# Second layer's first gate product set: S1 moved to second place, with T1's low part made from even tiles and a kept copy

## The reference, cut to what matters

```python
def rmsnorm(x, g):
    xf = x.astype(jnp.float32)
    y = xf * lax.rsqrt(jnp.mean(xf * xf, axis=-1, keepdims=True) + EPS)
    return (y * g.astype(jnp.float32)).astype(x.dtype)

def ffn_half(x, g, wg, wu, wd):
    h = rmsnorm(x, g)
    return x + 0.5 * ((jax.nn.silu(h @ wg) * (h @ wu)) @ wd)
...
def layer(h, pos, cache, ...):
    h = ffn_half(h, n1, w1g, w1u, w1d)
    z = rmsnorm(h, nm) @ w_in
    m, st = token_mix(z, ...)
    h = h + m @ w_out
    h = ffn_half(h, n2, w2g, w2u, w2d)
```

## Time and profile before

| | |
|---|---|
| median of 3 runs | 2104.92 us |
| profiled execution, and its span | 2107.2 us, 2105.4 us |
| granted clock of TensorE over the span | 0.992 |
| TensorE busy | 2054.5 us, 98% |
| VectorE busy | 1675.6 us, 80% |
| ScalarE busy | 978.2 us, 46% |
| GpSimd busy | 362.7 us, 17% |
| the place of the change | 1056 to 1074 us of the span |

### The profile page before, as it was taken

One profiled execution on the slowest core, in us unless ns is written; L12 is line 12 of the kernel. 1 busy time (PEld: TensorE's weight loads), 2 busy tenths in 40 slices (PEclk: granted clock), 3 DMA queues, 4 the chain that ended last, 5 costly groups with the idle time before them and its releaser, 6 DMA issues. The chain is left out here.

```text
span 2105.4 us, 41112 instructions
## 1 busy us (share of the span) xinstructions
PE 2054.5 (98%) x15435; PEld 1980.3 (94%) x15435; DVE 1675.6 (80%) x2481; ACT 978.2 (46%) x1772; POOL 362.7 (17%) x219
## 2 busy tenths in 40 slices
PE   8999999999999999999989999999999899999998
PEld 7999999999778999999989999999987699999998
DVE  5999997655655999998889999975555579999975
ACT  6544453324435544463465555433354364444532
POOL 0322200141110222200022221002402112222000
PEclk9999999999998999999999999999999999999999
DMA  4323323351111233322223322325312013332331
GB/s 130 96 84 100 97 73 104 94 129 40 44 42 61 83 98 100 94 87 84 76 81 99 100 82 88 98 76 130 94 42 63 31 61 101 100 99 78 94 93 63
DMA packets 236727, 178.35 MB, mean 85 GB/s; under 512 B 35808, under 2 KB 231616, under 8 KB 236608
## 3 DMA queue, kind: packets, MB, share of 16 engines
q1 hardware_dynamic: 231712, 170.36, 27.1%
q10 hardware_dynamic: 4896, 6.36, 1.1%
HBM read 170.12 MB, written 3.62 MB: 83 GB/s over the span
## 5 line engine op out<-in xcount | busy, mean ns | idle before, releaser
L1431 PE MATMUL pair<-t_parts,chunk_high 128*128 128x288 f32 x4592 | 916.8, 295 | 6.3 <-POOL chunk_low L794 2.6
L1431 PEld LDWEIGHTS pair<-t_parts,chunk_high 128*128 128x128 f32 x4592 | 736.7, 188 | 8.0 <-POOL chunk_low L794 3.2
L1431 PE MATMUL pair<-t_parts,chunk_low 128*128 128x288 f32 x2296 | 677.8, 295 | 0.0
L1431 PEld LDWEIGHTS pair<-t_parts,chunk_low 128*128 128x128 f32 x2296 | 431.4, 188 | 0.0
L794 POOL TENSOR_TENSOR chunk_low<-set_raw,chunk_high 128x512 fp32r<-128x512 f32 x164 | 240.6, 1477 | 869.6 <-ACT chunk_high L893 869.6
L893 ACT ACTIVATE chunk_high<-chunk_sum 128x512 fp32r<-128x512 f32 x328 | 203.8, 630 | 371.8 <-DVE chunk_sum L1982 190.4
L788 POOL TENSOR_TENSOR w_low<-raw,w_high 128x1024 fp32r<-128x1024 f32 (+2 forms) x48 | 114.7, 2394 | 626.8 <-ACT w_high L841 626.8
L1994 DVE TENSOR_TENSOR chunk_low<-chunk_sum,chunk_high 128x512 fp32r<-128x512 f32 x328 | 214.6, 695 | 9.3 <-ACT chunk_high L893 1.9
L1378 PE MATMUL pair<-hidden_high,w_high 128*128 128x288 f32 x896 | 193.6, 298 | 6.5 <-DVE hidden_low L2257 6.4
L1378 PE MATMUL pair<-hidden_high,w_low 128*128 128x288 f32 x896 | 191.8, 296 | 0.0
L1378 PE MATMUL pair<-hidden_low,w_high 128*128 128x288 f32 x896 | 191.6, 295 | 0.0
(11 more groups left out here) (300 smaller groups left out, 3742.1 us busy)
## 6 DMA issues: line engine op xcount, KB each, us to landing
set_raw<-in_w_up_dram SPq DMA_DIRECT2D x44, 1024.0 KB, 5.3
set_raw<-in_w_gate_dram SPq DMA_DIRECT2D x44, 1024.0 KB, 5.3
raw<-in_w_down_dram SPq DMA_DIRECT2D x64, 448.0 KB, 3.8
down_raw<-in_w_down_dram SPq DMA_DIRECT2D x16, 1024.0 KB, 5.4
raw<-in_w_in_dram SPq DMA_DIRECT2D x20, 512.0 KB, 4.0
raw<-in_w_in_dram SPq DMA_DIRECT2D x16, 256.0 KB, 3.8
raw<-in_w_out_dram SPq DMA_DIRECT2D x8, 512.0 KB, 3.5
raw<-in_w_out_dram SPq DMA_DIRECT2D x16, 256.0 KB, 4.0
```

What stands on the lines that cost most here:

```text
L1431: mm = nc.tensor.matmul(out, c[:, j, p, :], tr[p // 2][:, seat(p), x, t, :], start=p == 0 and n == 0, stop=p == KP - 1 and n == 2)
```

## The change

Three edits, all for the one set where `first` holds. TensorE goes through the products in the order A11, S1, A12, S2, S3, S4, A22. ScalarE and VectorE wait for three used chunks instead of two or three where they want A12's or S1's chunk buffer. And VectorE's list in `down_to_gate_up` is written anew: S1 and S2 are summed, T1 of the last pair is copied into the place of its T2 and its low is made, and S1's low is made, all before `plain_out(7)`; `odd_sums` then reads T1 from the copy.

```diff
--- before.py
+++ after.py
@@ -102,6 +102,12 @@
 PRODUCTS = {A11: (B11, ALONE, None), A12: (B21, FIRST, 0), S1: (T1, SECOND, 0), S2: (T2, FIRST, 1),
             S3: (T3, SECOND, 1), S4: (B22, THIRD, 0), A22: (T4, THIRD, 1)}
 C11, C12, C21, C22, U2, U4, U3, P1 = range(8)
+FIRST_ORDER = [A11, S1, A12, S2, S3, S4, A22]
+
+
+def used_after(j, first):
+
+    return 3 if first and j in (A12, S1) else j + 1
 
 
 def is_plain(layer, w):
@@ -535,6 +541,7 @@
         d_low = sem("down_chunk_low")
         d_left, d_out, d_scaled, h_part = sem("down_left"), sem("down_out"), sem("down_scaled"), sem("h_part")
         dt_sum, dt_high, dt_ready = sem("down_t_sum"), sem("down_t_high"), sem("down_t_ready")
+        t1_kept = sem("t1_kept")
         h_by_act, plain_low = sem("h_by_act"), sem("plain_low")
 
         def stand_alone(eng):
@@ -926,7 +933,7 @@
                     last = isinstance(i, int) and i == MP - 1 and b == 1
 
                     def done(j):
-                        act.wait_ge(chunk_used, 7 * q + (j + 1))
+                        act.wait_ge(chunk_used, 7 * q + used_after(j, opens and b == 0))
 
                     done(A11)
                     if last:
@@ -1403,7 +1410,7 @@
                     opens = isinstance(i, int) and i == 0
                     first = opens and b == 0
                     after_plain = isinstance(i, int) and i == 1 and b == 0 and is_plain(layer, w)
-                    for j in range(7):
+                    for j in FIRST_ORDER if first else range(7):
                         t, pair, half = PRODUCTS[j]
                         if j in (A11, A12):
                             pe.wait_ge(low_by_pool, 2 * q + {A11: 1, A12: 2}[j])
@@ -2003,13 +2010,13 @@
                 nc.vector.scalar_tensor_tensor(out=tf[p // 2][:, seat(p), 1, T1, :], in0=h[:, 2 * p, HALF:], scalar=gain_of(gain_col + 2 * p), in1=tf[p // 2][:, seat(p), 1, B11, :] if x is None else x,
                                                op0=ALU.mult, op1=ALU.subtract).then_inc(t_sum, 1)
 
-            def odd_sums(ph, p, gain_col, x=None):
+            def odd_sums(ph, p, gain_col, x=None, t1=None):
 
                 n = ph * (4 * KP) + 4 * p
                 x21, x22 = (tf[p // 2][:, seat(p), 1, B21, :], tf[p // 2][:, seat(p), 1, B22, :]) if x is None else x
                 dve.wait_ge(t_odd, ph * KP + (p + 1))
                 dve.wait_ge(t_sum, n + 1)
-                nc.vector.tensor_tensor(tf[p // 2][:, seat(p), 1, T2, :], x22, tf[p // 2][:, seat(p), 1, T1, :], ALU.subtract).then_inc(t_sum, 1)
+                nc.vector.tensor_tensor(tf[p // 2][:, seat(p), 1, T2, :], x22, tf[p // 2][:, seat(p), 1, T1, :] if t1 is None else t1, ALU.subtract).then_inc(t_sum, 1)
                 dve.wait_ge(t_sum, n + 2)
                 nc.vector.tensor_tensor(tf[p // 2][:, seat(p), 1, T4, :], x21, tf[p // 2][:, seat(p), 1, T2, :], ALU.subtract).then_inc(t_sum, 1)
                 nc.vector.scalar_tensor_tensor(out=tf[p // 2][:, seat(p), 1, T3, :], in0=h[:, 2 * p, HALF:], scalar=gain_of(gain_col + 2 * p), in1=x22,
@@ -2070,7 +2077,7 @@
                     finish = b == 0 and not opens
 
                     def done(j):
-                        dve.wait_ge(chunk_used, 7 * q + (j + 1))
+                        dve.wait_ge(chunk_used, 7 * q + used_after(j, first))
 
                     after_plain = isinstance(i, int) and i == 1 and b == 0 and is_plain(layer, w)
                     if not first and not after_plain:
@@ -2296,14 +2303,19 @@
                         if p == 1:
                             plain_out(6)
                     even_sum(ph, 3, count, gain_col)
+                    combine(q, 0, S1)
                     t_low(ph, 3, B11)
-                    combine(q, 0, S1)
+                    combine(q, 0, S2)
+                    last_t1 = tf[1][:, seat(3), 1, T1, :]
+                    dve.wait_ge(t_sum, ph * (4 * KP) + 13)
+                    nc.vector.tensor_copy(tf[1][:, seat(3), 1, T2, :], last_t1).then_inc(t1_kept, 1)
+                    dve.wait_ge(t1_kept, layer + 1)
+                    dve.wait_ge(t_high[2], ph * KP + 4)
+                    nc.vector.tensor_tensor(tr[1][:, seat(3), 1, T1, :], last_t1, tr[1][:, seat(3), 0, T1, :].bitcast(F32), ALU.subtract).then_inc(t_ready[T1], 1)
+                    chunk_low(q, 0, S1)
                     plain_out(7)
-                    combine(q, 0, S2)
-                    odd_sums(ph, 3, gain_col)
+                    odd_sums(ph, 3, gain_col, t1=tf[1][:, seat(3), 1, T2, :])
                     t_low(ph, 3, B21)
-                    chunk_low(q, 0, S1)
-                    t_low(ph, 3, T1)
                     square_of(4)
                     combine(q, 0, S3)
                     combine(q, 0, S4)
```

## The result

The changed kernel took 2110.2 us, the median of 11 runs (2106.14 to 2111.72). 11 runs of the kernel before beside them had a median of 2105.55 (2104.49 to 2107.76). The ratio is 1.0020 with a 95% interval of 1.0011 to 1.0028: +2.3 to +5.9 us. The forecast was 2107.3 us in a range of 2104.4 to 2108.9: the sign was right, the time lies 1.3 us above the range.

A forecast was written before the change was run, and what follows sets the result against it. VectorE's instruction list was taken as the kernel's clock from 1056 to 1089. A shift of +2.46 us with the copy held, rounded down to +2.4, on the median 2104.92 gave 2107.3 us, range 2104.4 to 2108.9.

The forecast's parts named there:

- the base: Starting time of the sum: median of the timed runs of the kernel before, 2104.92 us.
- the spread given to it: Half a microsecond allowed in the range for the spread of runs, 2104.55 to 2105.55 us.
- the difference carries over: Profiled execution, 2107.2 us, lies 2.3 us above the median; the same distance was assumed after the change.
- The mechanism's +2.46 us at S2: On TensorE, S2 starts at 1068.78 instead of 1066.32, since VectorE waits for ScalarE's square of tile 4.
- The list of VectorE: VectorE's instructions put ahead of tile 7's residual delay it 2.57 us, and S2's low by 2.46 us.
- Each sign that was named: Residual near 1062.2, VectorE waiting 0.8 us, TensorE about 3 us; wrong if residual before 1060.5 or S2 before 1067.3.
- The order in which the port was given: GpSimd's low of A12 takes the shared SBUF port at 1058.08, ahead of VectorE's copy, which waits until 1059.37.
- The copy: New VectorE copy of T1 ahead of tile 7's residual, taken as 0.36 us; bounds 0.1 us each way.
- The waits for used chunk buffers: On ScalarE and GpSimd, the changed waits become later counts that were long reached, with order unchanged.
- Rival 1: GpSimd does not get in between VectorE's SBUF instructions; S2 starts 1.4 us late, 2106.3 us; chance 0.17.
- Rival 2: TensorE decides, S1's 1.6 us fills the wait before A12's last pair, 2103.3 us; chance 0.10.
- Rival 3: TensorE's clock falls during its waits between 1063.6 and 1068.8, 1 us more, 2108.3 us; chance 0.18.

The follow-up runs named there:

- VectorE's list alone: Changed kernel's new VectorE list with TensorE's product order of the kernel before: section 34.29 us, median 2109.75 against 2106.37 us, ratio 1.0012.
- TensorE's order alone: TensorE's new product order with VectorE's list of the kernel before: section 32.35 us, median 2107.55 against 2106.37 us, ratio 1.0009.
- second series: The changed kernel timed again, unaltered, beside the kernel before: median 2109.7 against 2106.2 us, ratio 1.0013 (1.0004 to 1.0022).
- The delay alone: Kernel before plus five dependent VectorE instructions ahead of the last pair's odd sums: section 34.22 us, median 2108.59 against 2105.85 us, ratio 1.0013.
- the GpSimd kernel: Changed kernel with GpSimd's low of A12 waiting for tile 7's residual: section 33.73 us, median 2110.8 against 2106.47 us, ratio 1.0021.
- the fully filled one: Changed kernel with 41 unused matmuls in the set's waits and 11 more at the second set's end: 2111.48 against 2106.2 us, ratio 1.0027.

## Why the forecast was right in its mechanism and too low in its number

**The step that failed is the base, and with it the spread given to it.** The sum took +2.4 us from the median of three runs, 2104.92, by way of a profiled execution 2.3 us above it, with the words that "the difference carries over", and gave the spread half a microsecond. The mechanism's +2.46 us at S2 measured +2.20. What remains of the miss beyond the base is partly open, as told below.

**The list of VectorE: right.** Forecast +2.57 us for the residual, measured +2.32; for S2 +2.46, measured +2.20. Each sign that was named is there: VectorE waits 0.77 us for the square (0.8 forecast), TensorE 2.87 us for S2's low (3.0), the residual is done after 1060.5, S2 starts after 1067.3. VectorE's list alone shows the whole of it. The order in which the port was given was off by one instruction. GpSimd's request came in S2's sum (1056.92 to 1057.61); forecast was that it gets in ahead of the copy. The copy ran first, in 0.30 us, and GpSimd then held T1's low, 1.40 instead of 0.46 us. Both ways end in one held instruction; as measured it is 0.25 us cheaper. The copy was a term of 0.36 us, 0.06 too large. The waits for used chunk buffers that change are ScalarE's and VectorE's, not GpSimd's as the prediction has it; no term rests on that. The Trainium skill's rule in "SBUF — State Buffer", section "SBUF: two separate sides", that an fp32 copy takes the same lock, fits: GpSimd's 1.3 us, counted back from its end at 1058.95, began at 1057.65, when the copy was all but through. All eight executions in which this list stands unchanged up to the residual show the same: the copy 0.30 us, GpSimd 1.83 to 1.86, T1's low 1.40 to 1.43. That is not a proof, since no run has the copy and GpSimd's work side by side.

**Rival 1, no lock by GpSimd: refuted.** T1's low took 1.40 instead of 0.46 us. Forecast price 1.1 us for the lock on S2's path. Moving GpSimd away gives back 0.94 us at the residual and 0.6 us in the section.

**Rival 2, TensorE decides: refuted.** VectorE's list alone lengthens the section as much as the whole change; with TensorE's order alone a wait of 4.57 us moves it by 0.25 us.

**Rival 3, the clock: wrongly told, but not what the change cost.** It was told as a condition that holds or doesn't, with a chance of 0.18 and a price of 1 us, and the forecast's own sum had no clock term because the earlier trace rows show 1.00. The clock did fall, in each of the four executions of the changed kernel; but it also fell in the section in three of four of the kernel before, whose first execution was the exception. The fall cost 0.7 us in one of four after and in two of four before, so it adds nothing to the mean difference of the section. The price was near: where it cost something the mean's product came 1.74 us late (1.5 forecast) and 1.1 us of it were hidden (0.5 forecast). The single execution of before was no evidence that the stretch is free of it, and it held more falls than the one named: its granted share is 0.51 from 641 to 655 and 0.52 from 1675 to 1689.

**The base: too low.** "2104.92 plus the sum" took three runs of a kernel whose runs reach from 2103.64 to 2109.74. Its median is 2105.55 and 2105.85 us in series of 11 and 15 runs and 2106.2 to 2106.5 in those of 27 to 33. With +2.4 on the latter the forecast would have been about 2108.7, inside the changed kernel's runs. That is 0.6 to 1.5 us of the miss of 2.9. Nor is there a fixed distance between a profiled execution and the median: it was 2107.2 against 2105.55 for the kernel before, 2108.74 against 2110.2 for the changed one. The distance of 2.3 us was scatter, and the forecast carried it over as if it were a term. The range's lower end, 2104.4, left 1.4 us more room than rival 1 and half a microsecond ask for; the room was needed above.

**What is left: some 1.5 us, open.** The medians differ by 3.5 us (second series) to 4.65 us (first), the section by 2.0 to 2.2 us. By the ratios it is +4.2 us (2.3 to 5.9) and +2.7 us (0.8 to 4.6), so the section's 2.2 lies inside the second interval and just under the first: the excess itself is hardly clear of noise. In the means of four executions the excess is 1.05 us ahead of the section, which nothing in the change can reach and which I take for scatter, and 0.56 us behind it. The fall near 1575 has the right size, 1.5 to 1.6 us, and shows in three of four against none of four; with four of each that is a hint. It isn't brought by a late arrival (above: 1577.28 with it and 1577.29 without). The delay alone and VectorE's list alone ran without it, the GpSimd kernel and the fully filled one with it. These two are the slowest by their medians, but the GpSimd kernel's execution with the fall was its fastest, so this is no evidence either. What brings it stays open. The range gave half a microsecond to the spread of runs; it needed more than 2.

## What to carry to other kernels

Where one engine is full and another waits for it, read a reordering from the full engine's list: count what is put ahead of the instruction that a third engine waits for (here the residual), and follow that engine's answer back into the list. A product moved into a hole gained nothing here, since its operands come from the engine that made the hole. For an effect of 0.1%, take the base from many runs, give the range their spread, do not carry over the distance of one profiled execution from the median, and treat the clock as a cost that comes and goes in both kernels.

## What the runs showed of the hardware

- One and the same kernel has its falls of the clock in different places from one execution to the next, and a fall costs what lies in it: nothing where TensorE waits for VectorE anyway or the mean's product comes up to 1.0 us late, 0.7 us where that product comes 1.7 to 1.8 us late, 1.5 us at 1090 where TensorE is at work nearly all the time:

```profile
1088.00:1094.00 6.00, 4.43 (x23) 4.09 (x22) 5.14 (x8) 4.29 (x8) 0.00 (x0) 0.75 0.21 48
```

  (the kernel with VectorE's list alone; 1.49 us later behind this stretch than where it doesn't fall).
- Matmuls in the waits went with a clock of 1.00 all through the section in four executions of four; without them it was 1.00 in one of fifteen. The 11 runs of the changed kernel were no faster for it: 2109.58 against 2109.7 us by itself.
- An fp32 copy of 128x288 within SBUF took 0.30 us on VectorE. GpSimd's low of A12 was issued 0.4 us before this copy started and took 1.83 instead of 1.29 us; the instruction that it held (1.40 instead of 0.46 us) was the one behind the copy, not the copy.
